# Cross attention on one core: transposed probabilities and values split in high and low parts, outputs as products in three passes

## The reference

```
q = rmsnorm((h @ wq) per head, gq);  k = rmsnorm((m @ wk) per head, gk);  v = (m @ wv) per head
s = einsum('bshd,bmhd->bhsm', q, k) * 256 ** -0.5
p = softmax(s, axis=-1)
o = einsum('bhsm,bmhd->bshd', p, v)      # 4 heads of 256 columns, 512 tokens, 256 memory rows
return o @ wo
```

## Time and profile before

| what | value |
|---|---|
| time, median of 3 runs | 2725.95 us (2724.42 to 2727.76) |
| the profiled execution | 2724.47 us, of it the span 2722.7 us |
| granted TensorE clock over the span | 1.000 |
| busy in the span | PE 99%, PEld 87%, DVE 70%, POOL 60%, ACT 52% |
| cross attention with its projections on PE | from about 2265 to 2375 us in the span |
| matmul passes that the change replaces (line 3068) | 32, from 2307.4 to 2358.5 us |

### The profile page before, as it was taken

How to read it: one execution, slowest core, us unless ns; L and a number is a source line. 1 busy time by engine, 2 the same in 40 slices (tenths; PEclk the granted TensorE clock), 3 DMA queues, 4 the chain that set the end, 5 groups by cost and what they waited for, 6 DMA issues and landing times.

```text
span 2722.7 us, 47674 instructions
## 1 busy us (share of the span) xinstructions
PE 2705.9 (99%) x17250; PEld 2355.8 (87%) x17250; DVE 1915.5 (70%) x3043; ACT 1408.3 (52%) x2246; POOL 1625.3 (60%) x922
## 2 busy tenths in 40 slices
PE   9999999999999999999999999999999999999999
PEld 8998878999889998888999886665688888799988
DVE  6778667677857778535778947589788464467773
ACT  6555366555635555444555544566444444455552
POOL 6776545677657775444877553167533373377763
PEclk9999999999999999999999999999999999999999
DMA  4333422233332333332333341112222342123332
GB/s 146 118 113 92 130 78 93 93 108 108 100 117 93 108 108 113 110 105 78 109 108 123 91 129 55 55 55 70 85 71 78 101 154 78 55 94 108 110 114 86
DMA packets 80698, 268.09 MB, mean 98 GB/s; under 512 B 11168, under 2 KB 13216, under 8 KB 80560
## 3 DMA queue, kind: packets, MB, share of 16 engines
q1 hardware_dynamic: 77904, 262.01, 30.0%
q10 hardware_dynamic: 2656, 4.26, 0.5%
HBM read 263.09 MB, written 2.10 MB: 97 GB/s over the span
## 4 chain that ended last, share of the span: by engine, by line
PE 95%; DVE 3%; ACT 1%; issue 1%; DMA 0%; POOL 0%; ACTq 0%; SPq 0%; DVEq 0%
PE bank L499 15%; PE bank L500 15%; PE bank L503 15%; PE bank L819 12%; PE bank L821 12%; PE bank L820 12%; PE bank L602 1%; PE bank L604 1%; PE bank L603 1%; PE bank L2468 1%; PE bank L906 1%; PE bank L905 1%; PE bank L904 1%; PE bank L3336 1%; PE bank L3068 1%
## 5 line engine op out<-in xcount | busy, mean ns | idle before, releaser
L494 POOL TENSOR_TENSOR ring_lo<-w_stage,ring_hi 128x1024 fp32r<-128x1024 f32 (+2 forms) x166 | 393.2, 2382 | 422.0 <-ACT ring_hi L463 343.2
L487 POOL TENSOR_TENSOR ring_lo<-w_stage,ring_hi 128x1024 fp32r<-128x1024 f32 x108 | 267.7, 2485 | 370.0 <-ACT ring_hi L463 370.0
L979 POOL TENSOR_TENSOR ring_lo<-w_stage,ring_hi 128x1024 fp32r<-128x1024 f32 x196 | 363.2, 1853 | 157.2 <-ACT ring_hi L1117 157.2
L463 ACT ACTIVATE ring_hi<-w_stage 128x1024 fp32r<-128x1024 f32 (+2 forms) x274 | 273.3, 1014 | 178.2 <-PE bank L503 64.4
L499 PE MATMUL bank<-xg_hi,ring_hi 128*128 128x512 f32 x816 | 331.6, 406 | 1.1 <-POOL ring_lo L494 1.1
L821 PE MATMUL bank<-xg_hi,ring_lo 128*128 128x256 f32 x1176 | 325.2, 276 | 0.0
L821 PE MATMUL bank<-xsum,s_w 128*128 128x256 f32 x1176 | 325.1, 276 | 0.0
L819 PE MATMUL bank<-xg_hi,ring_hi 128*128 128x256 f32 x1176 | 325.1, 276 | 0.0
L820 PE MATMUL bank<-xg_lo,ring_hi 128*128 128x256 f32 x1176 | 325.1, 276 | 0.0
L820 PE MATMUL bank<-xsum,s_w 128*128 128x256 f32 x1176 | 325.1, 276 | 0.0
L819 PE MATMUL bank<-xsum,s_w 128*128 128x256 f32 x1176 | 325.1, 276 | 0.0
(11 more groups left out here) (604 smaller groups left out, 7446.0 us busy)
## 6 DMA issues: line engine op xcount, KB each, us to landing
w_stage<-w_up SPq DMA_DIRECT2D x220, 512.0 KB, 4.2
w_stage<-w_down SPq DMA_DIRECT2D x80, 512.0 KB, 3.8
w_stage<-merge SPq DMA_DIRECT2D x36, 512.0 KB, 3.6
w_stage<-w_down SPq DMA_DIRECT2D x40, 384.0 KB, 3.3
w_stage<-hg_qfg SPq DMA_DIRECT2D x12, 512.0 KB, 3.5
w_stage<-rec_r SPq DMA_DIRECT2D x8, 512.0 KB, 3.8
w_stage<-rec_y SPq DMA_DIRECT2D x8, 512.0 KB, 3.6
w_stage<-rec_out SPq DMA_DIRECT2D x8, 512.0 KB, 3.6
```

Source lines behind the costliest of these rows:

```text
L463: act.activation(w_hi[:, r, 0:w], w_stage[:, r, 0:w], ACT.Copy).then_inc(w_hi_ready, 1)
L487: pool.tensor_tensor(w_lo[:, r, 0:w], w_stage[:, r, 0:w], f32(w_hi[:, r, 0:w]), ALU.subtract).then_inc(w_lo_ready, 1)
L494: pool.tensor_tensor(w_lo[:, r, 0:w], w_stage[:, r, 0:w], f32(w_hi[:, r, 0:w]), ALU.subtract).then_inc(w_lo_ready, 1)
L979: pool.tensor_tensor(wb_lo[:, r, cs], w_stage[:, r, cs], f32(wb_hi[:, r, cs]), ALU.subtract).then_inc(w_lo_ready, 1)
```

## The change

`xprobT` becomes two tiles, `xprobT_hi` (written by ACT's copy) and `xprobT_lo` (PSUM minus the high part, on DVE). `vx` gets `vx_hi` (two ACT copies of 128x1024 at the head of `act_cross`) and `vx_lo` (two DVE subtractions of 128x1024 at the head of `dve_cross`, in the place of `vx`). Each output product of plain float32 becomes three of `F32R`. The release of bank 6 (`att_tc`) moves from ACT's copy to DVE's subtraction. Two semaphores of an earlier stage, `fox_hi` and `fox_lo`, which stand at 4 (`FOX_TILES`) by then, carry the new signals.

```
+    s1_down_at = cursor[0]
...
-    xprobT = place("xprobT", [P, 2, 2, T], at=R + 8 * KB)
+    xprobT_hi = place("xprobT_hi", [P, 2, 2, T], F32R, at=R + 8 * KB)
+    xprobT_lo = place("xprobT_lo", [P, 2, 2, T], F32R, at=R + 16 * KB)
+    vx_hi = place("vx_hi", [P, 2, D], F32R, at=s1_down_at + 12 * ASIDE)
+    vx_lo = place("vx_lo", [P, 2, D], F32R, at=R + 32 * KB)
...
@@ outputs(h), on PE
             elif h:
                 pe.wait_ge(xo_lo_ready, 2 * h)
+            else:
+                pe.wait_ge(fox_lo, FOX_TILES + 2)
             for i in range(2):
                 m = 2 * h + i
                 for kb in range(2):
-                    mm = pe.matmul(x_out_bank(m)[:], vx[:, kb, m * P:(m + 1) * P], xprobT[:, h % 2, kb, :],
-                                   start=kb == 0, stop=kb == 1)
+                    vh, vl = (v[:, kb, m * P:(m + 1) * P] for v in (vx_hi, vx_lo))
+                    ph, pl = (p[:, h % 2, kb, :] for p in (xprobT_hi, xprobT_lo))
+                    pe.matmul(x_out_bank(m)[:], vh, ph, start=kb == 0, stop=False)
+                    pe.matmul(x_out_bank(m)[:], vh, pl, start=False, stop=False)
+                    mm = pe.matmul(x_out_bank(m)[:], vl, ph, start=False, stop=kb == 1)
                 mm.then_inc(att_o, 1)
...
@@ dve_cross
+        def prob_low(n):
+            cs = (slice(None), n // 4 % 2, slice(None), slice(n % 4 * P, (n % 4 + 1) * P))
+            dve.wait_ge(fox_hi, FOX_TILES + 2 + n + 1)
+            dve.tensor_tensor(xprobT_lo[cs], bank[6][:, 0:2 * P].rearrange("p (k t) -> p k t", t=P), f32(xprobT_hi[cs]),
+                              ALU.subtract).then_inc(att_tc, 1)
+
+        for kb in range(2):
+            dve.wait_ge(fox_hi, FOX_TILES + kb + 1)
+            dve.tensor_tensor(vx_lo[:, kb, :], vx[:, kb, :], f32(vx_hi[:, kb, :]), ALU.subtract).then_inc(fox_lo, 1)
         q_tile(0)
         q_tile(1)
...
             if n < X_STEPS:
                 row_max(n)
+            if 0 <= n - 2 < X_STEPS:
+                prob_low(n - 2)
...
@@ act_cross
-            act.activation(xprobT[:, h % 2, :, qi * P:(qi + 1) * P], bank[6][:, 0:2 * P].rearrange("p (k t) -> p k t", t=P),
-                           ACT.Copy).then_inc(att_tc, 1)
+            act.activation(xprobT_hi[:, h % 2, :, qi * P:(qi + 1) * P], bank[6][:, 0:2 * P].rearrange("p (k t) -> p k t", t=P),
+                           ACT.Copy).then_inc(fox_hi, 1)
...
+        act.wait_ge(taken, layers["xv"].rbase + 4)
+        for kb in range(2):
+            act.activation(vx_hi[:, kb, :], vx[:, kb, :], ACT.Copy).then_inc(fox_hi, 1)
         for u in range(FIRST_UNITS):
             split(u)
```

More of the change, by code:

```diff
@@ L3006, in build @@
     X_NORM_AT = {2: 1, 6: 2, 11: 3}
+    FOX_TILES = 4
     def cross_head_out(n):
```

## The result

Nine runs of the changed kernel have a median of 2732.85 us (2731.93 to 2737.97), nine of the kernel before beside them 2727.76 (2724.42 to 2730.24). The ratio is 1.0024, with a 95% interval of 1.0016 to 1.0033: slower by 4.4 to 9.0 us, by 6.6 at the middle. The forecast was +4.3 us, a change within 0.2%, so the likeliest case was not the one that came. By the trace it was the second rival.

The account below looks back on a forecast made before the run. PE was taken to set the end, busy 95% of the span. Products -2.76, Q2's wait +5.9, `transposes(14)` +0.95 and the last head +0.2 gave +4.3 us: 2730.2 us, range 2725.5 to 2733.5.

Parts of the forecast that it names:

- the likeliest case: DVE takes turns with POOL, PE waits 5.9 us at Q2, clock stays; +4.3 us, 2729.3 to 2731.3, chance 0.42.
- the second rival: Clock falls in the wait before Q2, which begins at half rate; +5.8 to +8 us, 2731.8 to 2734, chance 0.31.
- The sum takes 0.: PE's clock in Q2's wait: no fall counted in the forecast; 1.5 us if it came as at the start, at most 5.45.
- Q2's delay: PE waits at Q2 for `q_tile(0)`, behind DVE's `vx_lo` taking turns with POOL: 5.9 us, bounds 2.0 and 6.4.
- The products of heads 0 to 2: Twelve `F32R` passes replace eight float32 passes on PE: 0.69 us less a head, 2.76 for all four heads.
- transposes(14): In slots 15 and 16 it waits longer for `prob_low(13)` behind `row_max(15)`: 0.95 us more, bounds 0.3 and 1.2.
- the last head: PE goes on with `o_lo` of tile 6, so up to 0.36 us of the products' saving is lost; 0.2 taken.
- the third: DVE and POOL do not meet, or once; Q2 waits 2.0 to 4.2 us, +0.4 to +2.6 in all; chance 0.18.
- the fourth: No wait at Q2, `q_tile(0)` not late: -1.6 us, 2724.3; chance 0.05.

Follow-up runs that it names:

- experiment 4: The changed kernel, but ACT makes the splits of Q3 and Q4 ahead of the two `vx_hi` copies; 2731.05 us, ratio to before 1.0015.
- experiment 6: The kernel of experiment 5, with five dummy float32 products on PE in slot 11 while it waits for DVE's query sum; 2723.45 us, ratio to before 0.9987.
- experiment 3: The changed kernel, but PE makes 22 dummy float32 products between Q1 and Q2, during the wait; 2730.27 us, ratio to before 1.0014.
- experiment 7: The changed kernel with `vx_lo` 0 left ahead of `q_tile(0)` and `vx_lo` 1 moved to slot 5; 2728.15 us, ratio to before 1.0004.
- experiment 5: The kernel of experiment 1, with `prob_low(13)` put ahead of `row_max(15)` in DVE's list in slot 15; 2722.54 us, ratio to before 0.9984.
- experiment 1: The changed kernel, but both `vx_lo` subtractions moved from ahead of `q_tile(0)` to slots 1 and 5; 2724.57 us, ratio to before 0.9993.
- experiment 2: The kernel before with only `vx_hi` and `vx_lo` made at their new places, used by nobody; 2734.19 us, ratio to before 1.0023.

## Why the prediction was wrong

**The step that failed** is the clock's: "The sum takes 0." I left a fall of the clock to the second rival at 0.31 because the idle 3.1 us at the span's end read 1.00 and no row had a longer gap. One trace was too few for that: in experiment 4's trace PE's last pass ends at 2725.35, and 2.65 us later, still inside the span, the clock reads 0.50 (2.8 us after the last pass in experiment 6):

```profile
2728.00:2728.40 0.40, 0.00 (x0) 0.50 0.00 0
```

An idle stretch of about 3 us can go either way. Here the fall cost 2.15 us in Q2, against the 1.5 that I took from the program's first stretch as the price if it came. Experiment 3 shows that the idle wait is the cause: the same wait, filled, leaves the clock at 1.00. The Trainium skill, "TensorE: Matmul & The Clock Gate", Part 1, says that idleness takes the engine back to the lower level; this case's traces agree (0.50 behind waits of 2.4, 4.0 and 5.7 us). By that rule my sum would have been the second rival's, on the side that came.

**Missed altogether:** the half rate in slot 12, 1.60 us, for which the sum has no term. The kernel before has the same slot 11, with the same wait of 1.1 us, at 1.00. Together the two falls make 3.75 us of the 7.73, and without them the stage is +4.06 (experiment 3).

**Right, with its size:** Q2's delay (5.9 forecast, 5.82 measured), and its mechanism: experiment 4 took one of POOL's turns away and 1.7 us of wait with it, experiment 7 left one subtraction and 2.4 us. The products of heads 0 to 2: 0.69 a head forecast, 0.70 measured; PE's timeline around head 1's outputs, for the earlier trace rows:

```profile
2331.47 0.38 PE L3062 MATMUL bank<-ident,xprob 128*128 128x128 f32 x2
...
2334.65 0.39 PE L504 MATMUL bank<-xg_lo,ring_hi 128*128 128x512 f32 x1
```

From the transposes to the second query pass it is 3.18 us now, 3.88 before. `transposes(14)`: 0.95 forecast, 1.00 measured, and experiment 5 shows that 0.58 of it comes from the place behind `row_max` in DVE's list. No other slot's transposes wait for `prob_low`.

**Small and off:** the last head. The kernel before (for the earlier trace rows) and the changed one, with the wait that follows in the kernel before:

```profile
2359.13 0.40 PE L500 MATMUL bank<-o_lo,ring_hi 128*128 128x512 f32 x1
...
2363.17 0.19 PEld L499 LDWEIGHTS bank<-o_hi,ring_hi 128*128 128x128 f32 x1 [0.44 <-POOL ring_lo L487]
```

```profile
2363.96 0.39 PE L3078 MATMUL bank<-xprobT_hi,vx_hi 128*128 128x512 f32 x1
...
2367.23 0.39 PE L504 MATMUL bank<-o_lo,ring_hi 128*128 128x512 f32 x1
```

From the head's first pass to the second one behind it, it is 3.66 us before and 3.27 now: 0.39 less instead of 0.70, so 0.31 is lost where I took 0.2. A little further on 0.28 comes back, where the kernel before waits for a weight unit's low part from POOL and the changed one hardly does. The sum has no term for that, and that the two nearly cancel is luck.

**The rivals:** the third (DVE and POOL meet once or not at all) and the fourth (no wait) are out by the timelines of the changed kernel. What the fourth would have given was -1.6; experiment 1 gives -1.87, near the terms that it was made of. That the range of the second rival, 2731.8 to 2734, and the forecast's whole range, 2725.5 to 2733.5, hold the median of 2732.85 is in part luck: the second rival had one fall in it, and the trace has two.

**Open:** why the clock fell in slot 12 of the changed kernel and of experiments 4 and 7, and not in the kernel before nor in experiments 1, 2, 3 and 5, with the same work of PE there. In all three traces with that fall the clock had fallen at Q2 before; in experiment 2 it had fallen at Q2 and did not fall in slot 12. Filling slot 11 did not tell.

## What to carry to other kernels

A preparation that is cheap by its engine's busy share is priced by what stands behind it in that engine's list: here two subtractions ahead of the one instruction that PE waited for cost 9.6 us in the traces, and nothing a few slots later. Where DVE subtracts two SBUF operands, look at what POOL does at the same time on the timeline, and count the turns. A wait put on PE is to be priced with the passes behind it at half rate, unless traces, more than one, show a wait of that length that left the clock up.

## What the runs showed of the hardware that was not expected

The granted clock was 0.50 behind a wait of only 2.4 us (experiment 7), while waits of 1.8 and 1.2 us in the traces left it at 1.00. A stretch with no single long wait can bring it too: slot 11's, whose longest wait is 1.1 us. Half-rate stretches also come in a stage that no kernel here changed. In experiment 5 the windows show one in the first attention (PE busy, passes, clock), which was at 1.00 over 1680 to 1695 us in the kernel before and the changed one:

```profile
1685.70:1688.90 3.20, 3.20 (x14) 0.50 0.00 0
```

It came in the traces of experiments 2, 3, 5 and 7. In slot 12 such a stretch cost 1.60 us, and the scatter between runs of one kernel, 5 us and more, goes with the clock: in experiment 1 the five runs with a granted clock of 1.000 took 2722.72 to 2723.36 us, the three with 0.999 took 2724.57 to 2725.12 and the three with 0.998 or 0.997 took 2727.93 to 2729.67. Where in those runs the clock fell, only a trace of each would show.
